# Gate, up and down products: one 512-column matmul for the rounded weight, 256 columns for its remainder

## The reference, cut to what matters

```python
def swiglu(h, w_gu, w_down):
    gate, up = jnp.split(h @ w_gu, 2, axis=-1)
    return (jax.nn.silu(gate) * up) @ w_down
...
    return x + swiglu(rmsnorm(x, norm_ffn), w_gu, w_down)
```

## Time and profile before

| | |
|---|---|
| Time, three executions | 902.39, 902.47, 903.47 us; median 902.47 us |
| Span of the profiled execution, first to last instruction | 901.0 us; the profile gives no other time for it |
| Instructions | 21291, of them 8676 matmuls |
| PE busy | 883.2 us, 98% of the span |
| VectorE, ScalarE, GpSimd busy | 639.2, 464.3, 116.4 us |
| Read from memory | 142.47 MB, 159 GB/s over the span |

### The profile page before, as it was taken

One profiled execution on the slowest core, in us unless ns is written; L12 is line 12 of the kernel. 1 busy time (PEld: TensorE's weight loads), 2 busy tenths in 40 slices (PEclk: granted clock), 3 DMA queues, 4 the chain that ended last, 5 costly groups with the idle time before them and its releaser, 6 DMA issues. The chain is left out here.

```text
span 901.0 us, 21291 instructions
## 1 busy us (share of the span) xinstructions
PE 883.2 (98%) x8676; PEld 848.8 (94%) x8676; DVE 639.2 (71%) x939; ACT 464.3 (52%) x732; POOL 116.4 (13%) x135
## 2 busy tenths in 40 slices
PE   7999999999999999999999999999999998999998
PEld 7989999999999988899999999999999887999998
DVE  6996866666566876767666666686987767757775
ACT  5774444444445566654444444368625544434453
POOL 2002300000022000050000015640008100000000
PEclk9999999999999999999999999999999999999999
DMA  8542555553556532254555445574433442243451
GB/s 333 203 160 96 185 187 178 180 177 134 180 192 219 182 106 104 79 187 166 178 176 185 168 161 177 194 255 160 180 123 131 138 118 72 95 141 139 153 177 48
DMA packets 23411, 144.52 MB, mean 160 GB/s; under 512 B 2968, under 2 KB 3224, under 8 KB 9648
## 3 DMA queue, kind: packets, MB, share of 16 engines
q1 hardware_dynamic: 22032, 140.26, 45.0%
q0 software_dynamic: 1168, 3.23, 1.5%
q10 hardware_dynamic: 144, 0.06, 0.0%
HBM read 142.47 MB, written 1.06 MB: 159 GB/s over the span
## 5 line engine op out<-in xcount | busy, mean ns | idle before, releaser
L548 PE MATMUL ps<-XH,hi 128*128 128x256 f32 x1304 | 374.4, 287 | 1.4 <-DVE XL L2018 0.7
L549 PE MATMUL ps<-XL,hi 128*128 128x256 f32 x1304 | 369.0, 283 | 0.0
L550 PE MATMUL ps<-XH,lo 128*128 128x256 f32 x1304 | 368.9, 283 | 0.0
L2004 DVE TENSOR_TENSOR lo<-raw,hi 128x1024 fp32r<-128x1024 f32 (+1 forms) x210 | 243.9, 1203 | 21.7 <-ACT hi L1435 8.3
L548 PEld LDWEIGHTS ps<-XH,hi 128*128 128x128 f32 x1304 | 250.1, 192 | 6.6 <-issue 4.8
L549 PEld LDWEIGHTS ps<-XL,hi 128*128 128x128 f32 x1304 | 250.2, 192 | 0.3 <-issue 0.2
L550 PEld LDWEIGHTS ps<-XH,lo 128*128 128x128 f32 x1304 | 250.1, 192 | 0.0
L548 PE MATMUL ps<-HH,hi 128*128 128x256 f32 x576 | 164.8, 286 | 3.4 <-DVE HL L2019 2.7
L549 PE MATMUL ps<-HL,hi 128*128 128x256 f32 x576 | 162.9, 283 | 0.0
L550 PE MATMUL ps<-HH,lo 128*128 128x256 f32 x576 | 162.9, 283 | 0.0
L1435 ACT ACTIVATE hi<-raw 128x1024 fp32r<-128x1024 f32 (+1 forms) x109 | 107.6, 987 | 30.4 <-DMA raw<-in_down 18.3
(11 more groups left out here) (376 smaller groups left out, 1157.5 us busy)
## 6 DMA issues: line engine op xcount, KB each, us to landing
raw<-in_wide SPq DMA_DIRECT2D x106, 1024.0 KB, 4.9
raw<-in_down SPq DMA_DIRECT2D x32, 704.0 KB, 4.0
BI<-bias_table POOLq DMA_DIRECT2D x16, 128.0 KB, 4.8
raw<-in_wide SPq DMA_DIRECT2D x3, 512.0 KB, 9.1
X<-in_x SPq DMA_DIRECT2D x1, 1024.0 KB, 13.4
WG<-in_group SPq DMA_DIRECT2D x1, 768.0 KB, 17.8
out<-X SPq DMA_DIRECT2D x3, 256.0 KB, 2.3
cmask<-in_masks POOLq DMA_DIRECT2D x1, 544.0 KB, 6.3
```

What stands on the lines that cost most here:

```text
L548: nc.tensor.matmul(dst, wh, xh, start=first, stop=False, skip_group_check=True)
L549: nc.tensor.matmul(dst, wh, xl, start=False, stop=False, skip_group_check=True)
L550: return nc.tensor.matmul(dst, wl, xh, start=False, stop=last, skip_group_check=True)
L2004: nc.vector.tensor_tensor(lo[:, s, a:b], raw[:, s, a:b], hi[:, s, a:b].bitcast(F32), ALU.subtract).then_inc(lo_ready, 1)
```

## The change

XH and XL become the two halves of one tensor X2, HH and HL those of H2. In `gu` and `down`, `product` is replaced by `wide_product`: the weight remainder times the upper tile goes into columns 0 to 255 of a bank, then the rounded weight times both parts of the tile, one matmul of 512 columns, into the whole bank. So columns 0 to 255 hold two of the three terms, columns 256 to 511 ("lower half") the third, and the two halves have to be added. Gate and up now take a bank each, so a unit of `gu` takes two banks: 6 and 7 for even units, 0 and 1 for odd ones. `down` takes banks 6 and 7 in turn.

ScalarE gets a new step `lower_terms`: behind `unit_done` it copies the lower halves of both banks into GU (128x512), ahead of its `split_hi` of unit u+2. VectorE's `hidden_in` waits for that copy, adds the upper halves (raises `evac_done`), waits for its own result and multiplies by RS. In `down` VectorE adds X and the two halves in two instructions instead of one.

```diff
--- before.py
+++ after.py
@@ -137,8 +137,8 @@
         arrival.close()
         lo = sb("lo", [P, SLOTS, UNIT], F32R)
         X = sb("X", [P, KD, T])
-        XH = sb("XH", [P, KD, T], F32R)
-        XL = sb("XL", [P, KD, T], F32R)
+        X2 = sb("X2", [P, 2, KD, T], F32R)
+        XH, XL = X2[:, 0, :, :], X2[:, 1, :, :]
         vec = sb("vec", [P, N_VEC])
         gfp = sb("gfp", [P, KD])
         fnsq = sb("fnsq", [P, KD])
@@ -162,8 +162,8 @@
         RC = sb("RC", [P, 2, 2])
 
         block1 = ExitStack()
-        HH = sb("HH", [P, KF, T], F32R, block1)
-        HL = sb("HL", [P, KF, T], F32R, block1)
+        H2 = sb("H2", [P, 2, KF, T], F32R, block1)
+        HH, HL = H2[:, 0, :, :], H2[:, 1, :, :]
         MK = sb("MK", [P, 2, 2, T], F32, block1)
         MV = sb("MV", [P, 2, 2, T], F32, block1)
         QM = sb("QM", [P, 2, T], F32, block1)
@@ -256,10 +256,14 @@
         SIG = sb("SIG", [P, 2, 2, T], F32, late)
         late.close()
 
-        ps = [ctx.enter_context(nc.psum_tensor(f"ps{i}", [P, 512], F32)) for i in range(6)]
+        front = ctx.enter_context(nc.psum_tensor("ps01", [P, 2, 512], F32))
+        ps = [front[:, 0, :], front[:, 1, :]]
+        ps += [ctx.enter_context(nc.psum_tensor(f"ps{i}", [P, 512], F32)) for i in range(2, 6)]
         both = ctx.enter_context(nc.psum_tensor("ps67", [P, 2, 512], F32))
         ps += [both[:, 0, :], both[:, 1, :]]
         PROJ, STAT, LOG, TRA, OUTP = ps[0:2], ps[2], ps[3:5], ps[5], ps[6:8]
+        DOWN = OUTP
+        GATE_UP = (both, front)
 
 
         loaded = [sem(f"loaded{i}") for i in range(SLOTS)]
@@ -268,6 +272,8 @@
         unit_done = sem("unit_done")
         evac_done = sem("evac_done")
         x_done = sem("x_done")
+        lower_in = sem("lower_in")
+        x_part = sem("x_part")
         xh_ready, xl_ready = sem("xh_ready"), sem("xl_ready")
         mh_ready, ml_ready = sem("mh_ready"), sem("ml_ready")
         hh_ready, hl_ready = sem("hh_ready"), sem("hl_ready")
@@ -549,6 +555,11 @@
                 nc.tensor.matmul(dst, wh, xl, start=False, stop=False, skip_group_check=True)
                 return nc.tensor.matmul(dst, wl, xh, start=False, stop=last, skip_group_check=True)
 
+            def wide_product(bank, wh, wl, x, first, last):
+
+                nc.tensor.matmul(bank[:, 0:T], wl, x[:, 0, :], start=first, stop=False, skip_group_check=True)
+                return nc.tensor.matmul(bank, wh, x, start=False, stop=last, skip_group_check=True)
+
             def channels(u, s, g, gp, rh, rl, k0=0, ready=None):
 
                 slot = s
@@ -719,10 +730,23 @@
             def gu(u0):
                 layer = 0 if u0 == U_GUA else 1
                 g0 = first_group(u0)
-                channels(u0, u0 % 4, g0, g0 % 2, XH, XL, 0, from_x(8 + 16 * layer))
+                ready = from_x(8 + 16 * layer)
+
+                def unit(u, s):
+                    bank_free(u + (g0 - u0))
+                    for m in range(2):
+                        half_ready(u, m)
+                        for k in range(KD):
+                            if m == 0 and isinstance(u, int) and u == u0:
+                                ready(k)
+                            c = slice((m * KD + k) * P, (m * KD + k + 1) * P)
+                            last = wide_product(GATE_UP[(s - u0) % 2][:, m, :], hi[:, s, c], lo[:, s, c], X2[:, :, k, :],
+                                                k == 0, k == KD - 1)
+                    last.then_inc(unit_done, 1)
+
+                unit(u0, u0 % 4)
                 stats(2 + 2 * layer, False)
-                over_units(pe, u0 + 1, N_GU - 1, lambda u, s: channels(
-                    u, s, u + (g0 - u0), (g0 + (s - u0)) % 2, XH, XL))
+                over_units(pe, u0 + 1, N_GU - 1, unit)
 
             def down(u0):
                 layer = 0 if u0 == U_DNA else 1
@@ -747,8 +771,8 @@
                             half_ready(u, 1)
                         c = slice(k * P, (k + 1) * P)
                         t = h * DN_TILES + k
-                        last = product(PROJ[(g0 + turn) % 2][:, 0:T], hi[:, s, c], lo[:, s, c],
-                                       HH[:, t, :], HL[:, t, :], h == 0 and k == 0, h == 1 and k == DN_TILES - 1)
+                        last = wide_product(DOWN[turn], hi[:, s, c], lo[:, s, c], H2[:, :, t, :],
+                                            h == 0 and k == 0, h == 1 and k == DN_TILES - 1)
                     last.then_inc(unit_done, 1)
 
 
@@ -1545,7 +1569,13 @@
                 layer = 0 if u0 == U_GUA else 1
                 m0 = N_GU * layer
 
+                def lower_terms(u, s):
+                    act.wait_ge(unit_done, u + 1)
+                    nc.scalar.activation(GU[:, s % 2, :, :], GATE_UP[(s - u0) % 2][:, :, T:2 * T],
+                                         ACT.Copy).then_inc(lower_in, 1)
+
                 def step(u, s, n):
+                    lower_terms(u, s)
                     split_hi(u + AHEAD, (s + AHEAD) % 4, n)
                     hidden(u, s)
 
@@ -1562,6 +1592,7 @@
 
                 split_hi(u0 + AHEAD, (u0 + AHEAD) % 4, UNIT)
                 rstd(2 + 2 * layer, False)
+                lower_terms(u0, u0 % 4)
                 hidden(u0, u0 % 4)
                 loop_units(u0 + 1, N_GU - 6, lambda u, s: step(u, s, UNIT))
                 for u in range(u0 + N_GU - 5, u0 + N_GU):
@@ -2191,12 +2222,13 @@
                     dve.wait_ge(table_stored, 16)
 
                 def hidden_in(u, s):
-                    dve.wait_ge(unit_done, u + 1)
-                    src = PROJ[(g0 + (s - u0)) % 2][:, :].rearrange("p (a b) -> p a b", a=2)
-                    nc.vector.tensor_tensor(GU[:, s % 2, :, :], src, twice(RS[:, 0, :]),
+                    dve.wait_ge(lower_in, u + (1 + m0 - u0))
+                    banks = GATE_UP[(s - u0) % 2]
+                    nc.vector.tensor_tensor(GU[:, s % 2, :, :], GU[:, s % 2, :, :], banks[:, :, 0:T],
+                                            ALU.add).then_inc(evac_done, 1)
+                    dve.wait_ge(evac_done, u + (g0 - u0 + 1))
+                    nc.vector.tensor_tensor(GU[:, s % 2, :, :], GU[:, s % 2, :, :], twice(RS[:, 0, :]),
                                             ALU.mult).then_inc(gate_in, 1)
-                    dve.wait_ge(gate_in, u + (1 + m0 - u0))
-                    dve.sem_inc(evac_done, 1)
 
                 def hidden_out(u, s):
                     b = s % 2
@@ -2241,8 +2273,10 @@
                     count = m + (8 + 16 * layer + 1)
                     if odd:
                         dve.wait_ge(unit_done, u + 1)
-                        src = PROJ[(g0 + turn) % 2][:, 0:T].rearrange("p (a b) -> p a b", a=1)
-                        nc.vector.tensor_tensor(tile(X, m), tile(X, m), src, ALU.add).then_inc(x_done, 1)
+                        upper, lower_ = (DOWN[turn][:, n * T:(n + 1) * T].rearrange("p (a b) -> p a b", a=1) for n in range(2))
+                        nc.vector.tensor_tensor(tile(X, m), tile(X, m), upper, ALU.add).then_inc(x_part, 1)
+                        dve.wait_ge(x_part, m + (8 * layer + 1))
+                        nc.vector.tensor_tensor(tile(X, m), tile(X, m), lower_, ALU.add).then_inc(x_done, 1)
                         dve.wait_ge(x_done, count)
                         dve.sem_inc(evac_done, 1)
                     late = isinstance(m, int) and m == KD - 1
```

## The result

The changed kernel takes 893.62 us (median of four executions, 891.23 to 897.93) against 902.43 for the kernel before beside it: ratio 0.9904, 95% interval 0.988 to 0.9927. It is faster by about 1%, where 2.4% was forecast, and just above the top of the range (893.5). The profiled execution, 891.23 us, has a span of 889.5 us, 11.5 less than before. The executions spread over 6.7 us, those of the kernel before over 1.3.

What follows compares the result with a forecast made beforehand. The prediction took the PE's matmul stream to bound the kernel. Products saving 25.3 us less 3.8 us of costs gave 21.5 us, so 902.5 us would fall to 881.0 us, with a range of 875 to 893.5 us.

Steps and rivals of the forecast that it cites:

- What bounds the kernel: Whole kernel: the rate of the PE's own matmul stream sets the time, 120 ns per 256 columns where columns need 106.7.
- The wide matmul: Gate, up and down: wide 216 ns plus narrow 120, so 336 ns a product instead of 360, saving 25.3 us.
- rival (a): All products: the 13 ns belong to each matmul, not the load; 347 ns a product, 892.0 us; chance 20%.
- The ring: Gate and up: evacuation loop over ScalarE and VectorE once a unit, 5.03 us, under the unit's 5.38, costing nothing.
- rival (c): Gate and up: the evacuation loop over both engines is longer, say 5.6 us, and limits the units; 890.9 us; chance 10%.
- rival (b): All products: the narrow matmul speeds up too, 325 ns a product; 869.5 us; chance 7%.
- Where cover ends: Starts and ends of the feed-forward stages: four places where added evacuation work delays the PE, 3.8 us together.
- (1): From gate and up into down: the PE's wait for the last HL grows by 1.4 us a layer, 2.8 us.
- (2): First unit of gate and up: tiles wait for XL, so six products gain nothing; 0.14 us, 0.3 in both layers.
- (3): First evacuation of gate and up: it waits for RS and may free the bank late; 0.2 us a layer, 0.4.
- (4): Behind down: the second add delays X; covered in the first layer, 0.3 us at the second layer's stats product.
- (d): All products: a wide matmul costs 240 ns, as two narrow ones, so only costs remain; 905.9 us; chance 7%.

Runs made afterwards that it cites:

- widths: Changed kernel with a tile's two parts adjacent and, behind each group's first product, wide matmuls of 320, 384, 448 or 256 columns by stretch: 858.46 us, one execution.
- loads: Changed kernel, tile parts adjacent, some weight loads halved to 64 columns; in the second layer's down both matmuls take 512 columns instead: 908.73 us, one execution.
- bf16 run: Changed kernel with a tile's two parts adjacent and all operands of the first layer's gate, up and down read as bf16: 888.54 us, one execution.
- again: The changed kernel measured once more without any edit: 894.65 us, ratio 0.992 to the kernel before.
- grouped: Changed kernel with the narrow matmuls of each half unit first, then its wide ones: 893.62 us, ratio 0.9899 to the kernel before.
- best: Changed kernel with narrow matmuls before wide ones in each half unit, and waiting for the last HL only before the product reading it: 889.67 us, ratio 0.9852.
- bestnear: Changed kernel with narrow matmuls before wide ones, the wait for the last HL only where read, and a tile's two parts adjacent: 891.16 us, ratio 0.9874.
- latewait: Changed kernel whose second down unit waits for the last HL only before its last product, which alone reads it: 890.41 us, ratio 0.9859.

## Why the prediction was wrong, step by step

**What bounds the kernel: right.** The PE's stream sets the time before and after, and columns alone do not make up its 120 ns.

**The wide matmul: wrong, and this is the step that decided.** It was put at 216 ns from the stats product, whose records stand 0.215 us apart; it takes 230 ns in the better stretches and 236 in the others. I read the 13 ns as a load too long for 256 columns, which 512 would cover. Runs widths and loads show the opposite: the excess is the same, 26 to 27 ns for two matmuls, at every width from 256 to 512, and halving one load leaves it. It is a price for each matmul with its load, 13.3 ns in the mean, and the change removes one in three: 14.0 us and not 25.3. This was rival (a), with 20% and 892.0 us; the profiled execution came to 891.23. The warning stood in the trace: starts were 120 ns apart beside every neighbour. The loads' own records warned too: in the trace of the kernel before they last 192 ns for the rounded weight (L548) and 188 for the stats product (L634), with starts 120 and 215 ns apart, so that length alone did not set the 120. The stats product is of another type. That float32 matmuls there have 2 ns of excess and the rounded type 13 has no explanation in these runs; the bf16 run changed the type and the length of the loads together.

**Two ways of running: not foreseen.** A product takes 347 or 353 ns for a whole stretch, at the same clock. The profiled execution of the result was at or near 347 everywhere and came to 891.23 us, inside the range; the profiled one of run again had three of four stretches at 353 and came to 895.42. The median of 893.62 us lies 2.4 us above the first and just above the range, whose top was (a) plus little. That the executions in between had stretches at 353 is likely but not shown, since they have no trace, and differences outside the parts add 1 us or more of their own. In the traces of the grouped order (runs grouped, best and bestnear) the two layers take the same time to 0.03 us, so the two rhythms go with narrow and wide taking turns; what picks one for a stretch is open.

**The ring: right in kind, 5.03 us worked out, 5.1 to 5.2 measured.** Behind the first units VectorE is late and catches up; there its adds L2227 stand a ring apart (VectorE's timeline, then ScalarE's):

```profile
110.50 0.69 DVE L2227 TENSOR_TENSOR GU<-GU,ps 128x512 f32<-128x512 f32 x1
...
115.35 0.43 DVE L2243 TENSOR_TENSOR H<-GU,H 128x256 f32 x1 [0.83 <-ACT H L1591]
115.69 0.68 DVE L2227 TENSOR_TENSOR GU<-GU,ps 128x512 f32<-128x512 f32 x1
```

```profile
114.98 0.58 ACT L1574 ACTIVATE GU<-ps 128x512 f32<-128x512 f32 x1
```

The copy ends at 115.56, but the add starts only behind HL (L2243), which the sum had left out of the ring. Still the ring is under 5.38 as under 5.55, so it costs nothing, and rival (c) fell. Run widths shows it as the bound. There the PE needs 16 x (149 + 118) ns = 4.3 us for a unit of the first layer, but VectorE's adds (L2229 in that kernel) still stand 5.1 to 5.3 us apart, and the PE waits for `lo` as this line of its list of waits says:

```profile
PE ps L561 <- DVE lo L2037: 10.1, 27, 0.6
```

So at a product of 325 ns, a unit of 5.20, as under rival (b), the ring would have been the bound together with the PE.

**Where cover ends.** (1) The pause at the start of down: 1.25 us more a layer against 1.4, right; run latewait shows that it was on the path and can be had back. (2) 0.14 us a layer for the first products: about right. From its first product to the first of down, gate and up of the first layer takes 128.3 us before and 123.8 after, 4.5 saved where 352 products at 13.3 ns give 4.7. The last wait for XL ends 3.17 us after the first product started in the kernel before and 3.16 in the changed one, so the products ahead of it gained nothing. (3) The first bank is free when the PE wants it: the first add starts at 107.20 and takes 0.69 us, and the third unit starts at 108.35 without a wait. (4) Between the two parts 113.7 us pass before and after, and no PE wait for a bank or for the sums stands in the list, so nothing was found. With 14.0 us for the products, 2.5 for the pauses and some 0.3 for (2) the account gives 11.2, which is what the two parts lost. The costs were 2.8 us where 3.8 were put down: (3) and (4), 0.7 together, were not there, and (1) was 0.3 too large.

**Rivals (b) and (d)** fell: the narrow one stayed at 117 ns with rounded operands, and a wide one is cheaper than two narrow ones, though by 10 ns and not by 24.

## What to carry to other kernels

Where starts of matmuls stand further apart than their columns, don't take the gap for a hidden load that a longer stream will cover. Fewer matmuls with loads save the fixed price, here 13 ns each, and a row of another type is a bound on it only. When steps are put ahead of an engine's old work, look at the ends of a stage, where the last result is waited for, and let each wait stand at the first instruction that reads the data: here that gave 3.2 us, about a third of what the whole change gave. And where executions differ by as much as the effect, as here by the clock and the rhythm, compare the stretch that was changed in the traces and not the medians alone.

## What was not expected of the hardware

Rounded-type matmuls of 256 and 512 columns taking turns settle into one of two rhythms, 347 ns or a round of three products with 353 in the mean, at granted clock 1.00 in both, and keep it for tens of microseconds. Outside the slower rhythm, a pair of rounded-type matmuls costs 26 to 27 ns over its columns, 13.3 ns each in the mean, with 256 columns in the one and 256, 320, 384, 448 or 512 in the other (29 to 30 in the grouped order); a matmul of bf16 (read with a step of two, with loads of 96 ns in place of 189) 6.5 ns at 256 and 12 at 512.
